# Eleven modulation pieces leave the mixer of the first block and are folded by VectorE in the feed-forward

## The reference, cut to what matters

```
cond = silu(c)
for i in range(2):                      # layers of the second block
    mod = cond @ ada_w[i] + ada_b[i]    # (1, 1024) @ (1024, 6144)
    sh1, sc1, g1, sh2, sc2, g2 = split(mod, 6)
    h = rms_norm(x, norm1_g[i]) * (1 + sc1) + sh1
    ...
```

## Time and profile before

| | |
|---|---|
| median of 3 runs | 2401.33 us (2400.99 to 2404.18) |
| span of the profiled execution, first to last instruction | 2399.5 us |
| own time of the profiled execution beside its span | not listed; the three runs lie 1.5 to 4.7 us above the span |
| TensorE busy | 2162.0 us (90%), 9926 instructions |
| VectorE busy | 872.5 us (36%) |
| ScalarE, GpSimd busy | 439.2 us (18%), 263.3 us (11%) |
| mixer, feed-forward (from the timeline) | 0 to about 345 us, about 345 to 742 us |
| bytes moved by DMA | 586.99 MB, 245 GB/s |

### The profile page before, as it was taken

The page is one execution under the profiler, slowest core; times in us unless marked ns, Lnnn a source line. Parts: engine busy times, 40 slices in busy tenths (PEclk is TensorE's granted clock), DMA queues, the critical chain, the costliest instruction groups (busy, mean ns, idle before and its releaser), DMA issues. The chain is left out here.

```text
span 2399.5 us, 25420 instructions
## 1 busy us (share of the span) xinstructions
PE 2162.0 (90%) x9926; PEld 1250.5 (52%) x9926; DVE 872.5 (36%) x1710; ACT 439.2 (18%) x835; POOL 263.3 (11%) x508
## 2 busy tenths in 40 slices
PE   8999999999999998998887787799899988888786
PEld 4354448888877875463322232388554733222222
DVE  2255626666536449241111100463472411011114
ACT  2222411000002017111000000110482201000001
POOL 3122102000000002111111011000131111111110
PEclk9999999999999999999999899999999999999999
DMA  7558826222122114089999999811203699999997
GB/s 272 184 200 287 294 78 239 91 80 96 60 92 91 51 58 163 35 323 417 407 429 427 425 420 416 328 70 36 73 1 140 254 419 414 428 427 427 426 423 284
DMA packets 130470, 586.99 MB, mean 245 GB/s; under 512 B 18024, under 2 KB 29680, under 8 KB 105548
## 3 DMA queue, kind: packets, MB, share of 16 engines
q1 hardware_dynamic: 114912, 548.72, 57.2%
q0 software_dynamic: 14864, 36.76, 4.2%
q10 hardware_dynamic: 604, 0.27, 0.1%
HBM read 571.31 MB, written 30.65 MB: 251 GB/s over the span
## 5 line engine op out<-in xcount | busy, mean ns | idle before, releaser
L2522 PE MATMUL ps<-ring,arena 128*64 128x512 f32 x1920 | 454.6, 614 | 94.6 <-ACT arena L2571 51.9
L2522 PEld LDWEIGHTS ps<-ring,arena 128*64 128x64 f32 x1920 | 143.5, 141 | 375.2 <-issue 282.7
L2560 PE MATMUL ps<-ring,arena 128*64 128x512 f32 x928 | 230.6, 654 | 45.4 <-DMA ring<-in_expert_w_down 33.7
L2600 DVE TENSOR_TENSOR arena<-ps,arena 128x512 f32<-128x512 f32 x32 | 22.1, 692 | 518.4 <-PE ps L2522 518.4
L2560 PEld LDWEIGHTS ps<-ring,arena 128*64 128x64 f32 x928 | 77.3, 149 | 178.7 <-issue 163.3
L2605 DVE TENSOR_TENSOR arena<-ps,arena 128x1024 f32<-128x1024 f32 x30 | 36.7, 1225 | 308.2 <-PE ps L2560 308.2
L1183 PE MATMUL ps<-hT,ring 128*128 128x256 f32 x640 | 141.6, 379 | 0.0
L1183 PEld LDWEIGHTS ps<-hT,ring 128*128 128x128 f32 x640 | 121.5, 190 | 16.5
L2571 ACT ACTIVATE arena<-ps,mod 128x128 f32<-128x128 f32 x128 | 48.1, 456 | 331.0 <-PE ps L2512 331.0
L1183 PE MATMUL ps<-ring 128*128 128x256 f32 x480 | 106.9, 379 | 0.0
L1569 PE MATMUL ps<-ring 128*128 128x256 f32 x480 | 106.0, 379 | 0.0
(11 more groups left out here) (449 smaller groups left out, 3091.2 us busy)
## 6 DMA issues: line engine op xcount, KB each, us to landing
ring<-in_expert_w_gate SPq DMA_DIRECT2D x60, 2048.0 KB, 17.2
ring<-in_expert_w_up SPq DMA_DIRECT2D x58, 2048.0 KB, 17.6
ring<-in_expert_w_down SPq DMA_DIRECT2D x56, 2048.0 KB, 18.4
ring<-in_ada_w SPq DMA_DIRECT2D x24, 2048.0 KB, 10.9
ring<-in_diff_w_in SPq DMA_DIRECT2D x6, 2048.0 KB, 8.2
ring<-in_sb_w_in SPq DMA_DIRECT2D x6, 2048.0 KB, 16.5
ring<-in_ffn_w_gate SPq DMA_DIRECT2D x5, 2048.0 KB, 12.8
ring<-in_ffn_w_val SPq DMA_DIRECT2D x5, 2048.0 KB, 8.0
```

Of the source, the lines that this page charges most:

```text
L2522: mm = pe.matmul(k.ps[slots, 2 + kind, :], k.xT[:, c, slots], w[:, c, :], start=(c == 0), stop=(c == KD - 1))
L2560: mm = pe.matmul(k.ps[slots, 5 + half, :], k.hTt[:, c, slots], w[:, c, half * 512:(half + 1) * 512], start=(c == 0), stop=(c == KH - 1))
L2600: dve.tensor_tensor(k.hid[:, :], k.ps[:, 3, :], k.sg[:, :], ALU.mult).then_inc(m.hidden, 1)
```

## The change

Thirteen pieces stay in the mixer, the last of them the first of layer 1; the other eleven become 22 half pieces `h` of 256 columns (1 MB). `FIRST_ADA` and the four pieces behind `turn_outputs` go, and steps 8 to 10 have one piece each; step 11 keeps two. VectorE multiplies a half piece by `cond` chunk by chunk and adds the eight chunks (`mod_fold_vector`): half pieces 0 to 9 at the end of groups 2, 3, 6, 7, ... 18, 19, and two in each of down steps 0 to 5. TensorE sums the 128 partitions of two folded half pieces with a stationary matrix of ones (`mod_sums_tensor`), eleven times: at the start of groups 6, 10, 14, 18 and ahead of product 7 in down steps 1 to 7. ScalarE copies each result and writes two rows to HBM (`mod_row_scalar`). The half pieces use slot 3 of the ring, half each; the feed-forward's weights rotate over the other three slots. The columns of layer 1 are made by GpSimd behind `distances_gpsimd`. A few early semaphores are merged.

```diff
-ADA_PIECES = 24
+ADA_PIECES = 13
-FIRST_ADA = 4
-STEPS = (... (12, 2), (13, 2), (14, 2), (15, 2))
+STEPS = (... (12, 1), (13, 1), (14, 1), (15, 2))
...
-        if j in FIRST_JOBS[-FIRST_ADA:]:
-            modulate(ada)
...
-    for a in range(ada, ADA_PIECES):
-        unit(*todo.pop(0))
-        modulate(a)
...
+def mod_load(sp, k, h):
+    if h >= 2:
+        sp.wait_ge(k.s.mod_folded, h - 1)
+    elif h == 1:
+        sp.wait_ge(k.s.ffn_plain, 2)
+    ...
+    sp.dma_start(mod_buffer(k, h), rows_strided(k.ada_w[l])[:, :, c0:c0 + MOD_W])...
+
+def mod_fold_vector(dve, k, ch, step):
+    for h in MOD_FOLDED.get(step, ()):
+        dve.wait_ge(k.s.mod_loaded[h % 2], 16 * (h // 2 + 1))
+        ...
+        if h >= 4:
+            dve.wait_ge(k.s.mod_summed, h // 2 - 1)
+        part, acc = mod_buffer(k, h), k.mod_acc[h // 2 % 2][:, h % 2, :]
+        ch.link(dve.tensor_scalar(acc, part[:, 0, :], k.cvec[:, 0:1], None, ALU.mult))
+        for c in range(1, KD):
+            ins = dve.scalar_tensor_tensor(out=acc, in0=part[:, c, :], scalar=k.cvec[:, c:c + 1], in1=acc, op0=ALU.mult, op1=ALU.add)
+            if c < KD - 1:
+                ch.link(ins)
+        ins.then_inc(k.s.mod_folded, 1)
+
+def mod_sums_tensor(pe, k, step):
+    r = MOD_SUMMED[step]
+    if r:
+        pe.wait_ge(k.s.mod_taken, r)
+    pe.wait_ge(k.s.mod_folded, 2 * r + 2)
+    for g in range(2):
+        mm = pe.matmul(k.ps[32 * g:32 * g + 32, mod_bank(step), HALF_T:HALF_T + MOD_W], k.ones[:, 0:32], k.mod_acc[r % 2][:, g, :],
+                       start=True, stop=True, skip_group_check=True)
+    mm.then_inc(k.s.mod_summed, 1)
+
+def mod_row_scalar(act, k, step):
+    if step not in MOD_SUMMED:
+        return
+    r = MOD_SUMMED[step]
+    act.wait_ge(k.s.mod_summed, r + 1)
+    act.wait_ge(k.s.row_out, 16 * (4 + 2 * r))
+    act.copy(k.mod_row, k.ps[0:64, mod_bank(step), HALF_T:HALF_T + MOD_W]).then_inc(k.s.mod_taken, 1)
+    act.wait_ge(k.s.mod_taken, r + 1)
+    for g in range(2):
+        ...
+        act.dma_start(k.mod_dram[:, c0:c0 + MOD_W], k.mod_row[32 * g:32 * g + 1, :])...
...
 def ffn_tensor(pe, k):          # the start of a group; and in a down step, ahead of product 7:
+        if group in MOD_SUMMED:
+            mod_sums_tensor(pe, k, group)
...
+    pe.wait_ge(s.mod_taken, MOD_ROUNDS)
     for tt in range(TT):
...
 def ffn_scalar(act, k):
-    for half in range(2):
+    for step in range(DOWN_STEPS):
+        if step == 3:
+            act.wait_ge(s.ffn_prod, 3 * GROUPS_FFN + 1)
+            act.copy(k.down_part, k.ps[:, 0, :]).then_inc(s.ffn_first_out, 1)
+        mod_row_scalar(act, k, GROUPS_FFN + step)
+    for half in (1,):
         act.wait_ge(s.ffn_prod, 3 * GROUPS_FFN + 6 * half + 1)
-        if half:
-            act.wait_ge(s.ffn_evac, GROUPS_FFN + 2)
-        act.copy(k.down_part, k.ps[:, 7 * half, :]).then_inc(s.ffn_first_out, 1)
+        act.wait_ge(s.ffn_evac, GROUPS_FFN + 2)
+        act.copy(k.down_part, k.ps[:, 7, :]).then_inc(s.ffn_first_out, 1)
...
 def ffn_vector(dve, k, ch, a):
+        mod_fold_vector(dve, k, ch, group)
         if group == GROUPS_FFN - 2:
             low[0]()
             low[1](4)
...
         if step < DOWN_STEPS - 2:
             weight_sums_vector(dve, k, ch, GROUPS_FFN + step + 2)
+        mod_fold_vector(dve, k, ch, GROUPS_FFN + step)
```

More of the change, by code:

```diff
@@ L288, in job_order @@
 def job_order():
-    order, ada = list(FIRST_JOBS[:-FIRST_ADA]), iter(range(ADA_JOB, JOBS_1))
-    for j in FIRST_JOBS[-FIRST_ADA:]:
-        order += [j, next(ada)]
+    order, ada = list(FIRST_JOBS), iter(range(ADA_JOB, JOBS_1))
     for n, (j, pieces) in enumerate(STEPS):
@@ L1063, with mod_bank @@
 FIRST_HALF, LAST_HALF = slice(0, HALF_T), slice(HALF_T, T)
+MOD_W = 256
+MOD_SLOT = 3
+MOD_STEPS = 4
+MOD_ROUNDS = 2 * 6 * D // (2 * MOD_W) - ADA_PIECES
+MOD_FOLDED = {4 * n + i: (2 * n + i,) for n in range(1, 6) for i in (-2, -1)} | {GROUPS_FFN + s: (10 + 2 * s, 11 + 2 * s) for s in range(6)}
+MOD_SUMMED = {4 * r + 6: r for r in range(4)} | {GROUPS_FFN + 1 + r: 4 + r for r in range(MOD_ROUNDS - 4)}
+def mod_bank(step):
+    return 4 * (step % 2) + 2 if step < GROUPS_FFN else (7 if step < GROUPS_FFN + 4 else 6)
@@ new lines, in mod_sums_tensor @@
+def mod_sums_tensor(pe, k, step):
[16 more added lines that the diff above has]
+    for g in range(2):
+        c0 = ADA_PIECES * 512 + (2 * r + g) * MOD_W
+        act.dma_start(k.mod_dram[:, c0:c0 + MOD_W], k.mod_row[32 * g:32 * g + 1, :]).then_inc(k.s.row_out, 16)
@@ L1170, in ffn_tensor @@
             pe.wait_ge(s.ffn_evac, group - 1)
+        if group in MOD_SUMMED:
+            mod_sums_tensor(pe, k, group)
         for n in PRODUCTS:
+            if n == 7 and group in MOD_SUMMED:
+                pe.wait_ge(s.mod_taken, MOD_SUMMED[group] + 1)
             if n == 7 and group == 0:
@@ L1209, in ffn_tensor @@
                 pe.wait_ge(s.ffn_evac, GROUPS_FFN)
+            if step == 4 and n == 1:
+                pe.wait_ge(s.mod_taken, MOD_SUMMED[GROUPS_FFN + 3] + 1)
+            if n == 7 and group in MOD_SUMMED:
+                if step == 4:
+                    pe.wait_ge(s.ffn_evac, GROUPS_FFN + 2)
+                mod_sums_tensor(pe, k, group)
             if step == 4 and n in (2, 7):
@@ L1267, in ffn_scalar @@
             act.copy(k.first_product, k.ps[:, 4 * (group % 2) + 3, 0:HALF_T]).then_inc(s.ffn_first_out, 1)
+            mod_row_scalar(act, k, group)
         if group == 0:
@@ L2932, in modulation_gpsimd, with mod_columns_gpsimd @@
         pool.wait_ge(s.mod_steps, g)
-    pool.dma_start(k.mod_dram.rearrange("a (p n) -> p (a n)", p=P), k.mod_sum).then_inc(s.mod_landed, 16)
+    pool.dma_start(k.mod_dram[:, 0:ADA_PIECES * 512].rearrange("a (p n) -> p (a n)", p=P), k.mod_sum).then_inc(s.mod_landed, 16)
     pool.wait_ge(s.mod_landed, 32)
[L2935 to L2945, removed]
+def mod_columns_gpsimd(pool, k, l):
+    s = k.s
+    if l:
+        pool.wait_ge(s.row_out, 16 * (4 + 2 * MOD_ROUNDS))
+    for i, v in enumerate((0, 1, 3, 4)):
+        pool.dma_start(k.mod[:, l, i, :], k.mod_rows[l, v, :].rearrange("(p k) -> p k", p=P)).then_inc(s.mod_landed, 16)
+        pool.dma_start(k.modb[:, l, i, :], k.ada_b[l, v * D:(v + 1) * D].rearrange("(p k) -> p k", p=P)).then_inc(s.mod_landed, 16)
+    pool.wait_ge(s.mod_landed, 16 * (2 + 8 * (l + 1)))
+    pool.tensor_tensor(k.mod[:, l, :, :], k.mod[:, l, :, :], k.modb[:, l, :, :], ALU.add).then_inc(s.mod_steps, 1)
+    pool.wait_ge(s.mod_steps, 3 + MOD_STEPS * l + 1)
+    for i in (1, 3):
+        pool.tensor_scalar(k.mod[:, l, i, :], k.mod[:, l, i, :], 1.0, None, ALU.add).then_inc(s.mod_steps, 1)
+    pool.wait_ge(s.mod_steps, 3 + MOD_STEPS * l + 3)
     pool.wait_ge(s.gains_landed, 16 * 6)
-    for l in range(2):
-        for i, g in ((1, 2 + 2 * l), (3, 3 + 2 * l)):
-            ins = pool.tensor_tensor(k.mod[:, l, i, :], k.mod[:, l, i, :], k.gains[:, g, :], ALU.mult)
+    for i, g in ((1, 2 + 2 * l), (3, 3 + 2 * l)):
+        ins = pool.tensor_tensor(k.mod[:, l, i, :], k.mod[:, l, i, :], k.gains[:, g, :], ALU.mult)
     ins.then_inc(s.mod_steps, 1)
@@ L3192, in plan_first_block @@
     st.add([piece(st, gate, c0, P, 0, 2 * P), piece(st, value, c0, P, P, 2 * P)], s, "ffn_plain", 2)
+    st.rotate(0, 1, 2)
+    st.lend(MOD_SLOT, s, "mod_folded", 2 * MOD_ROUNDS)
     for group in range(0, GROUPS_FFN, 2):
@@ L3201, in plan_first_block @@
         st.add([piece(st, down[:, c0:c0 + n, :], half * 512, 512, chunks=n)], s, *used)
-    st.rotate(3, 0, 1, 2)
+    st.rotate(MOD_SLOT, *st.slots)
+    k.mod_loads_after = {k.ffn_piece + 1 + p: range(h, h + n)
+                         for p, h, n in ((0, 0, 2), (4, 2, 2), (6, 4, 2), (8, 6, 2), (10, 8, 2), (12, 10, 4), (13, 14, 4), (14, 18, 4))}
 def plan_attention(st, a, w_in, w_out, out_slots):
@@ L3384, in _ @@
                 k.stream1.load(sp, n)
+                for h in k.mod_loads_after.get(n, ()):
+                    mod_load(sp, k, h)
             moe_sync(sp, k, m, a, k.tails[0])
@@ L3398, in _ @@
             modulation_gpsimd(pool, k)
+            mod_columns_gpsimd(pool, k, 0)
             pool.wait_ge(s.ffn_pads, 2)
```

62 lines of the change are left out of this document (38 added, 24 removed).

## The result

The changed kernel takes 2410.4 us (median of 6 runs, 2408.33 to 2412.99) against 2401.75 us for the kernel before (6 runs, 2400.99 to 2404.18): 8.65 us (0.36%) between the medians. The measured ratio is 1.0029 (95% interval 1.0019 to 1.0039), which is 7.0 us (4.6 to 9.4); either way it is clearly slower. The profiled execution lasts 8.9 us longer than before, and the down matmuls behind the last down step, which started at 705.68 us, start at 714.48 us, 8.8 us later. So what these two traces differ by arose in the mixer and the feed-forward, and there I look.

What follows compares the result with a forecast made beforehand. TensorE was taken to bound mixer and feed-forward, VectorE's in-order list where it lags. Mixer -12.7 and feed-forward +15.6 gave +2.9 us on 2399.5, 2402.4 us; with 1.8 us for the median, 2404.2 us; range 2395 to 2411 us.

Steps and rivals of the forecast that it cites:

- The steps of the mixer: Mixer: pieces removed from the steps give back 1.86 us each, 7.4 us early and 5.6 us in steps 8 to 10.
- The four pieces at the end: End of the mixer: removing four pieces of 7.4 us gives back 1.8 us; about 5.3 us become TensorE idle time.
- The clock behind it: End of the mixer: a lower clock behind 4 to 5 us of idle time costs 2.1 us, ends 0 and 2.5.
- Sums: Feed-forward: eleven sums over partitions on TensorE, side by side, at 0.56 us each, cost 6.2 us (4.7 to 11).
- 2409 us, one after the other: Rival, feed-forward: the two matmuls of a sum don't run side by side, 4.8 us more; chance 0.12.
- Folds: Feed-forward, VectorE: a fold takes 4.1 us (3.4 to 6.3); groups 2 to 17 pay nothing, groups 18 and 19 do.
- The rival of a bound VectorE: Rival, down steps: VectorE becomes the bound above 4.9 us a fold, time 2418 us; chance 0.06.
- Down step 0: Down step 0: TensorE waits 4.1 us (2.8 to 8.6) for low[2] behind a fold, and the lower clock costs 2.1 us.
- Step 4: Down step 4: product 2 waits for the fifth addition of the first spread, 0.3 us.
- The end: Last down matmuls: ScalarE's later copy of bank 7 makes them wait 2.0 us, and a lower clock costs 0.9 us.
- the early 7.4 us not coming: Rival, early mixer: the chain of levels or a ring slot holds step 0, time 2411 us; chance 0.1.

Runs made afterwards that it cites:

- e1_squares: Changed kernel with VectorE's squares of tiles 2 and 3 moved behind the emptying of levels 7; 2404.79 us, ratio 1.0005 to the kernel before.
- e9_retimed: Changed kernel with four pieces taken out of mixer steps 1, 2, 3 and 11 and put behind the last four level units; 2400.22 us, ratio 0.9991.
- e11_before_cut: Kernel before with seven of the eight matmuls left out in each of the last four pieces; 2407.48 us in one run.
- e7_onesum: Changed kernel with each sum as one matmul with 128 stationary columns over the first folded half only; 2406.76 us in one run.
- e3_low: Changed kernel with the fold of group 18 behind low[0] and low[1], that of group 19 behind low[2] and low[3]; 2406.17 us, ratio 1.0016.
- e4_copy: Changed kernel with ScalarE's copy of bank 7 ahead of its row copy in down step 7; 2406.78 us, ratio 1.0014.
- e2_fill: Changed kernel with twelve spare 256-column matmuls ahead of the first out unit, results unused; 2406.21 us, ratio 1.001.

## Why the prediction came out as it did, step by step

**The steps of the mixer: right.** 13.0 us were forecast to the last level units and 12.8 came. L504 has 208 records, the turn is at 96.74 (forecast 96.5) and waited for nothing but its place in the list; 0.67 us went to a half job ahead of it, which waited for ScalarE (L609), a wait that I had not listed.

**The four pieces at the end give only 1.8 us: right.** The `out` units start 14.6 us sooner (forecast 14.8) behind 5.22 us of idle time (5.3), because VectorE's list is the bound there.

**The clock behind it: this is the step that failed.** I took 2.1 us for "an idle time of 4 to 5 us". It cost about 6.7: 4.5 in the `out` units (9.4 against 5.0 us), 1.7 in the projection (22.3 us from its start to the next turn against 20.6), 0.5 in the next stage (this last part varies by itself, as the end of this document shows). Two things were wrong. The price came from the earlier trace rows, where 384- and 512-column matmuls follow the idle time and the clock returns within some 5 us; here the work behind it was matmuls of 64 and 128 columns, over which it stayed low for 9.4 us of full work. And the idle time of 5 us was not needed: in e1_squares the longest is 0.87 us, and its `out` units take the same 9.4 us. What the change took away was not only time on TensorE but the wide matmuls between the last small units; that these pieces decide over the clock there, e9_retimed (put back, clock at 1.00) and e11_before_cut (seven eighths taken from the kernel before, clock at 0.50, behind 2.71 us of idle time) show from both sides. Which property of what is left lets it fall stays open: no run here separates the width of the matmuls from their rows or from the gaps between them.

**Sums: mechanism right, size off.** 0.75 to 0.76 us each instead of 0.56, eleven times: 8.4 instead of 6.2. They run side by side, so the rival "2409 us, one after the other" did not happen, though the time came out within 2 us of it, which is chance; my 0.13 us for the switch was what a piece costs beyond its two rounds, and that a sum pays no more was an assumption. The Trainium skill (TensorEngine Tiling (Array Packing), Key Properties) says that a change of mode drains TensorE; e7_onesum agrees that a change costs time on either side of the narrow pair (0.09 and 0.11 us, 0.33 us in all at most), but no run shows a drain as such.

**Folds: right.** 0.35 + 3.61 us, 3.91 from start to start, forecast 4.1; a 256-column multiply-add takes 485 ns on average, as estimated. Groups 2 to 17 pay nothing but the sums: 3.0 us over four. The rival of a bound VectorE (4.9 us a fold) fell with that; VectorE is never idle from 659 to 694 us, but it idles 2.7, 2.2 and 2.4 us ahead of the weight sums at 623, 636 and 649 us, and its lateness reaches TensorE nowhere behind step 0: the wait for L1442 at the end is ScalarE's, for which VectorE itself had idled 11.17 us. That rival's time was also added up wrongly: its own terms, five steps at 2.8 us and 4.5 more in step 0, give about 2423 us and not 2418.

**Down step 0: right in place.** The wait is 3.49 us (forecast 4.1), the clock behind it 3.0 us (2.1). Here the matmuls behind it have 256 columns, and the loss is near the 2.4 us worked out from the earlier trace rows. With both in place the wait and the clock cost 6.5 us together, 6.2 in the sum.

**Step 4: 0 us (forecast 0.3)**, probably since the wait in step 0 gave VectorE the time; e3_low, without that wait, has 1.7 us there.

**The end: a wait of 1.62 us (2.0), no low clock (0.9).** The cause was right: e4_copy removes exactly that.

Together: mixer -7.9 instead of -12.7, feed-forward +16.7 instead of +15.6. The miss of 5.9 us is 4.6 of clock at the mixer's end, 2.2 of sums, 0.9 of clock in step 0 and 0.2 in the start of the `out` units, less 2.2 in the waits of steps 0 and 4 and the wait and clock at the end; 0.2 is left over. The chance of 0.3 for slower was too small, since no rival let the clock cost more than 2.5 us at one place. That the range held the time is luck: its upper end came from rivals (the early 7.4 us not coming, the sums not side by side) of which none happened, and what filled their place was the clock, which no rival had at this price.

## What to carry to other kernels

Before you take filler away from TensorE, ask two things of the stretch: what its neighbours wait for (filler that lies in the shadow of another engine's list costs little, so take it from where TensorE is the bound), and what is left of TensorE's work there: in this kernel the clock fell where only small matmuls and short gaps were left. Look at the granted clock of the stretch after such a change. A price for the low clock that is read behind wide matmuls did not hold here for small ones. Where work is moved onto an in-order list, put it behind what a busy engine waits for, and look one wait further, since the wait that you remove may have been time in which the list caught up.

## What the runs showed of the hardware that I had not expected

- The granted clock fell to 1.2 GHz in the middle of level units with no idle time above 0.87 us (e1_squares, at about 262 us), and it was still at 0.50 after 9.4 us of back-to-back 64- and 128-column matmuls. With twelve 256-column matmuls ahead of them (e2_fill) it came back within their own 7.5 us.
- One and the same idle time of 4.24 us, ahead of the same sixteen matmul records at the start of the stage behind the mixer, costs a different amount in each program: those records take 7.86 us before, 8.38 in the change (341.49 us), and in e9_retimed:

```profile
331.24 6.88 PE L250 MATMUL ps<-hT,ring 128*128 128x384 f32 x16 [4.24 <-issue]
```

  A single row is therefore no firm price for what a low clock costs: between 6.88 and 8.38 us lie 1.5 us with nothing changed there.
- Two side-by-side matmuls of 32 stationary and 256 moving columns between full ones cost 0.33 us more than one full-width matmul in their place (0.76 against 0.43 us, e7_onesum).
